# Layer norm with shifted statistics: partial mean ahead, squares summed among the output tiles

## Chip, cores and metric

The kernel runs on one core of a Trainium2 chip. The metric is the device time of one launch in microseconds; the median of several executions is compared.

## What is computed

One inference step of a trunk of four layers over 384 tokens (128 context, 256 latent) of width 1024. A layer is a token mixer (gated MLP, SSD scan, HGRN2 scan, gated MLP again) and a mixture of 16 experts. Each of the eight sub-layers ends in a layer norm:

```
def layer_norm(x, g, b):
    mu = mean(x); var = mean(square(x - mu))
    return (x - mu) * rsqrt(var + 1e-5) * g + b

for li in range(4):
    sh1, sc1, g1, sh2, sc2, g2 = modulation(cond, w_mod[li], b_mod[li])
    h = x * (1 + sc1) + sh1
    x = layer_norm(ALPHA * x + g1 * mixer(h), ln_g[li, 0], ln_b[li, 0])
    h = x * (1 + sc2) + sh2
    x = layer_norm(ALPHA * x + g2 * moe(h), ln_g[li, 1], ln_b[li, 1])
```

## The kernel before

Activations lie transposed: 128 features on the partitions, 8 tiles (`KD`) of 384 tokens (`T`). `x`, `y` (the residual sum), `h32` (the modulated input of the next sub-layer) and the pair `hh`, `hl` (high and low part of it for two-part products) are all [128, 8, 384]. Every engine has a program of its own, written out by hand; order is by program order on an engine and by counting semaphores between engines. A norm is numbered q = 2 x layer for the one behind the mixer and 2 x layer + 1 for the one behind the experts.

**Weights.** SP loads 1 MB chunks into four buffers (`raw`); load c waits until chunk c - 4 has been used. Most chunks are split: ScalarE copies the high part (`whi`), POOL subtracts it (`wlo`, L1341), TensorE multiplies three times (L1408 to L1410). Chunks of `w_mod` are summed by VectorE alone, four instructions a chunk into `macc` (`mod_chunk`, L1672 and L1675), and their end frees the buffer.

**Out projection of a mixer** (`out_tiles`). TensorE makes eight output tiles m, in banks m % 4 of PSUM, from one chunk each (gated MLP and SSD) or half a chunk (HGRN2). After a tile VectorE adds it into `y` (`residual`, L1734, which raises `y_ready`); in layers 0 and 1 VectorE does the `mod_chunk` m ahead of the residual of tile m, in layer 3 one ahead of every second tile, in layer 2 likewise. The order of loads is w_mod chunk m, then out chunk m. Tile 7 is followed on TensorE by `mod_sum` (L1442, 32 small matmuls) in mixer projections. Behind tile m TensorE does the mean step m - 1 (`mean_step`, L1450: y tile times a matrix of 1/1024, summed in bank 6). Behind the experts the projection has the same form (L1632, L1633, banks m % 3) without chunks.

**Norm.** When the mean is complete, VectorE subtracts it from all of `y` in four instructions (L1715), ScalarE squares each pair of tiles (L1225, `ln_sq`), TensorE sums the squares in bank 5 (`variance`, L1458), ScalarE takes the root (L1227, in seven of eight norms with an ACT_TABLE_LOAD ahead), VectorE the reciprocal (L1718). Then comes a loop over the tiles: VectorE multiplies (L1720) and writes `h32` in two segments of 128 and 256 tokens (`modulate`, L1705), ScalarE writes `x` (L1231) and, behind the experts, `hh` (L1235), from which POOL makes `hl` (L1354).

**Who comes next.** Behind the first norm of a layer TensorE computes the router from `h32` (L1536, three token tiles in banks 4 to 6, each with `claim`), transposes `h32` (L1527) and gathers. `claim(b, name, value)` makes TensorE wait, before it writes bank b again, for the event that the bank's last user has registered.

Of the kernel before, what the change touches and what calls it, by code (L numbers as in the profile page):

```python
# [28 lines left out]
P = 128  # L29
# [112 lines left out]
def trunk(nc, A, O):  # L142
# [11 lines left out]
    with ctx:  # L154
# [54 lines left out]
        sq = ar("ln_sq", [P, KD, T], F32, 0)  # L209
# [98 lines left out]
        def bank(b):  # L308
# [6 lines left out]
            h32_ready hh_ready hl_ready y_ready mean_done diff_ready sq_ready var_done std_ready norm_ready x_ready  # L315
# [889 lines left out]
        def _(act):  # L1205
# [16 lines left out]
            def layer_norm(q, last=False):  # L1222
                for j in range(4):
                    act.wait_ge(S["diff_ready"], 4 * q + j + 1)
                    act.activation(sq[:, 2 * j:2 * j + 2, :], y[:, 2 * j:2 * j + 2, :], ACT.Square).then_inc(S["sq_ready"], 1)  # L1225
                act.wait_ge(S["var_done"], q + 1)
                act.activation(std[:, :], bank(5), ACT.Sqrt, bias=eps[:, 0:1]).then_inc(S["std_ready"], 1)  # L1227
                l, w = q // 2, q % 2
                for k in range(KD):
                    act.wait_ge(S["norm_ready"], 8 * q + k + 1)  # L1230
                    act.activation(x[:, k, :], y[:, k, :], ACT.Identity, scale=c_("lng", (2 * l + w) * 8 + k),  # L1231
                                   bias=c_("lnb", (2 * l + w) * 8 + k)).then_inc(S["x_ready"], 1)
                    if w and not last:
                        act.wait_ge(S["h32_ready"], 8 * (q + 1) + k + 1)
                        act.activation(hh[:, k, :], h32[:, k, :], ACT.Copy).then_inc(S["hh_ready"], 1)  # L1235
# [161 lines left out]
        def _(pe):  # L1397
# [48 lines left out]
            def mean_step(q, k):  # L1446
                pe.wait_ge(S["y_ready"], 8 * q + k + 1)
                if k == 0:
                    claim(6, "diff_ready", 4 * q + 4)
                ins = pe.matmul(bank(6), mean_d[:, :], y[:, k, :], start=(k == 0), stop=(k == KD - 1))  # L1450
                if k == KD - 1:
                    ins.then_inc(S["mean_done"], 1)

            def variance(q):
                claim(5, "std_ready", q + 1)
                for k in range(KD):
                    pe.wait_ge(S["sq_ready"], 4 * q + k // 2 + 1)
                    ins = pe.matmul(bank(5), mean_d[:, :], sq[:, k, :], start=(k == 0), stop=(k == KD - 1))  # L1458
                ins.then_inc(S["var_done"], 1)

            def out_tiles(l, rhi, rlo, halves, ready, count):

                q = 2 * l
                for m in range(KD):
# [7 lines left out]
                    if m:  # L1472
                        mean_step(q, m - 1)
                mean_step(q, KD - 1)
# [42 lines left out]
            def experts(l):  # L1517
# [15 lines left out]
                for k in range(KD):  # L1533
                    pe.wait_ge(S["h32_ready"], 8 * q + k + 1)
                    for t in range(NT):
# [91 lines left out]
                for m in range(KD):  # L1627
# [7 lines left out]
                    if m:  # L1635
                        mean_step(q, m - 1)
                mean_step(q, KD - 1)
# [4 lines left out]
            for l in range(DEPTH):  # L1642
# [6 lines left out]
                variance(2 * l)  # L1649
                experts(l)  # L1650
                variance(2 * l + 1)
# [3 lines left out]
        def _(dve):  # L1655
# [47 lines left out]
            def modulate(src, k):  # L1703
                for c, a, b in SEGS:
# [4 lines left out]
            def layer_norm(q, last=False):  # L1709
# [3 lines left out]
                dve.wait_ge(S["mean_done"], q + 1)  # L1713
                for j in range(4):
                    dve.tensor_tensor(y[:, 2 * j:2 * j + 2, :], y[:, 2 * j:2 * j + 2, :],  # L1715
                                      bank(6).unsqueeze(1).to_broadcast([P, 2, T]), ALU.subtract).then_inc(S["diff_ready"], 1)
                dve.wait_ge(S["std_ready"], q + 1)
                link(dve.reciprocal(rstd[:, :], std[:, :]))  # L1718
                for k in range(KD):
                    dve.tensor_tensor(y[:, k, :], y[:, k, :], rstd[:, :], ALU.mult).then_inc(S["norm_ready"], 1)  # L1720
                    if not last:
                        dve.wait_ge(S["norm_ready"], 8 * q + k + 1)
                        modulate(y, k)
# [7 lines left out]
            def residual(l, m, src, g_tile):  # L1731
# [4 lines left out]
                ins.then_inc(S["y_ready"], 1)  # L1736

# [269 lines left out]
```

## Time and profile before

| | us |
|---|---|
| Median of 3 runs | 3290.02 (3288.75 to 3301.81) |
| Profiled execution | 3285.35 |
| Its span on the core | 3283.6 |
| TensorE busy | 2724.3 (83%) |
| VectorE busy | 1518.5 (46%) |
| ScalarE busy | 744.5 (23%) |
| POOL busy | 802.0 (24%) |

TensorE's busy time counts overlapping matmuls and says little alone. The profile's timeline, read around each norm, shows which engine waits for which; the granted clock of TensorE (1.00 is 2.4 GHz, 0.50 is 1.2 GHz) stands in the last columns of a table by stretches. An fp32 matmul shows as two records.

### The profile page before, as it was taken

To read this page: it belongs to the slowest core of one execution; us is meant where nothing else is said; L and a number is where in the kernel's file an instruction comes from. 1 tells how busy PE (TensorE), PEld (TensorE's weight loads), DVE (VectorE), ACT (ScalarE), POOL (GpSimd) and SP (SyncE) were. 2 spreads that over 40 slices of the span, in tenths; PEclk is the share of its full clock that TensorE was granted. 3 is DMA by queue.
4 is the path that set the end of the run, shared out by engine and by line. 5 is a ranking of instruction groups with operands and counts; after the bars stand their busy time and mean duration, and the time that the engine had idled before them with its cause. 6 is when DMAs were issued, how large, how long until landed. Compare 5 with 4: busy or idle time off the path is not lost.

```text
span 3283.6 us, 30539 instructions
## 1 busy us (share of the span) xinstructions
PE 2724.3 (83%) x11846; PEld 1982.1 (60%) x11846; DVE 1518.5 (46%) x2423; ACT 744.5 (23%) x1252; POOL 802.0 (24%) x501
## 2 busy tenths in 40 slices
PE   1788998887986778889898876678888889989997
PEld 1688853445975667744347865567544469975444
DVE  7546532234546766522234567767322332662002
ACT  0132220002442332300013332332100033321101
POOL 2255200002442234100003555633000025630000
PEclk9889889898897889799998875578999989989999
DMA  6534447783320114278782420013588824335883
GB/s 218 169 113 129 141 154 281 274 289 116 106 90 26 52 52 144 74 267 297 267 282 89 135 68 4 5 41 116 177 285 285 292 95 134 114 118 178 297 301 114
DMA packets 291854, 524.42 MB, mean 160 GB/s; under 512 B 9472, under 2 KB 141056, under 8 KB 291328
## 3 DMA queue, kind: packets, MB, share of 16 engines
q1 hardware_dynamic: 288256, 519.33, 46.8%
q10 hardware_dynamic: 3456, 3.15, 0.3%
q8 instruction: 95, 1.56, 0.2%
q14 instruction: 47, 0.39, 0.0%
HBM read 517.73 MB, written 4.72 MB: 159 GB/s over the span
## 4 chain that ended last, share of the span: by engine, by line
PE 61%; DVE 19%; DMA 9%; issue 5%; ACT 3%; POOL 2%; SPq 0%; ACTq 0%; DVEq 0%
PE ps L1596 14%; PE ps L1611 10%; DMA raw<-moe_w_down 6%; DVE macc L1675 6%; PE ps L1408 5%; PE ps L1409 5%; PE ps L1410 5%; PE ps L1442 3%; PE ps L627 2%; PE ps L1458 2%; PE ps L1431 1%; PE ps L1432 1%; PE ps L1433 1%; POOL wlo L1341 1%; DVE h L1705 1%
## 5 line engine op out<-in xcount | busy, mean ns | idle before, releaser
L1341 POOL TENSOR_TENSOR wlo<-raw,whi 128x1024 fp32r<-128x1024 f32 x202 | 528.2, 2630 | 1709.4 <-ACT whi L1213 1709.4
L1596 PE MATMUL ps<-raw,xg 128*128 128x512 f32 x1536 | 696.3, 597 | 0.0
L1596 PEld LDWEIGHTS ps<-raw,xg 128*128 128x128 f32 x1536 | 285.8, 192 | 323.6 <-issue 321.8
L1611 PE MATMUL ps<-raw,hidt 128*128 128x512 f32 x768 | 389.4, 655 | 109.9 <-DMA raw<-moe_w_down 107.7
L1675 DVE SCALAR_TENSOR_TENSOR macc<-raw,cond_s,macc 128x1024 f32<-128x1024 f32 x336 | 459.7, 1430 | 9.0 <-DMA raw<-w_mod 9.0
L1886 DVE SCALAR_TENSOR_TENSOR hid<-ps,cws,sg 128x256 f32<-128x256 f32 x96 | 46.5, 484 | 780.0 <-ACT sg L1306 780.0
L1611 PEld LDWEIGHTS ps<-raw,hidt 128*128 128x128 f32 x768 | 157.3, 209 | 329.9 <-issue 193.3
L1408 PE MATMUL ps<-hh,whi 128*128 128x384 f32 x832 | 293.4, 353 | 35.2 <-POOL wlo L1341 19.3
L1213 ACT ACTIVATE whi<-raw 128x1024 fp32r<-128x1024 f32 x202 | 207.0, 1054 | 400.7 <-DMA raw<-gmlp_w_out 115.1
L1410 PE MATMUL ps<-hh,wlo 128*128 128x384 f32 x832 | 284.4, 342 | 0.0
L1409 PE MATMUL ps<-hl,whi 128*128 128x384 f32 x832 | 284.4, 342 | 0.0
L1280 ACT ACTIVATE hidt<-ps 128x256 f32<-128x256 f32 x96 | 36.8, 383 | 871.2 <-PE ps L1586 871.2
L1431 PE MATMUL ps<-whi,hh 128*128 128x256 f32 x480 | 145.2, 302 | 66.1 <-POOL wlo L1341 57.5
L1408 PEld LDWEIGHTS ps<-hh,whi 128*128 128x128 f32 x832 | 161.6, 194 | 45.6 <-POOL wlo L1341 20.9
L1409 PEld LDWEIGHTS ps<-hl,whi 128*128 128x128 f32 x832 | 161.9, 195 | 1.5 <-issue 0.5
L1410 PEld LDWEIGHTS ps<-hh,wlo 128*128 128x128 f32 x832 | 160.9, 193 | 0.0
L1432 PE MATMUL ps<-whi,hl 128*128 128x256 f32 x480 | 143.2, 298 | 0.0
L1433 PE MATMUL ps<-wlo,hh 128*128 128x256 f32 x480 | 143.0, 298 | 0.0
L1431 PEld LDWEIGHTS ps<-whi,hh 128*128 128x128 f32 x480 | 100.2, 209 | 68.6 <-POOL wlo L1341 58.4
L1014 PE MATMUL ps<-uw 128*128 128x128 f32 x336 | 92.4, 448 | 56.2 <-DVE uw L1123 56.2
L1442 PE MATMUL ps<-ones,macc 128*128 128x1 f32 x768 | 99.8, 264 | 45.8 <-DVE macc L1675 45.8
L1442 PEld LDWEIGHTS ps<-ones,macc 128*128 128x128 f32 x768 | 101.4, 214 | 51.9 <-issue 31.7
(322 smaller groups left out, 4261.5 us busy)
## 6 DMA issues: line engine op xcount, KB each, us to landing
raw<-moe_w_gu SPq DMA_DIRECT2D x192, 1024.0 KB, 6.1
raw<-w_mod SPq DMA_DIRECT2D x96, 1024.0 KB, 5.3
raw<-moe_w_down SPq DMA_DIRECT2D x96, 1024.0 KB, 5.5
raw<-gmlp_w_in SPq DMA_DIRECT2D x32, 1024.0 KB, 5.7
raw<-ssd_w_in SPq DMA_DIRECT2D x21, 1024.0 KB, 5.3
raw<-hgrn_w_in SPq DMA_DIRECT2D x20, 1024.0 KB, 5.2
raw<-gmlp_w_out SPq DMA_DIRECT2D x16, 1024.0 KB, 5.7
raw<-ssd_w_out SPq DMA_DIRECT2D x8, 1024.0 KB, 5.9
```

Source lines behind the costliest of these rows:

```text
L1213: act.activation(split_sub(whi, s0), raw_sub(s0), ACT.Copy).then_inc(S["hi_ready"], 1)
L1341: pool.tensor_tensor(split_sub(wlo, s0), raw_sub(s0), split_sub(whi, s0).bitcast(F32), ALU.subtract).then_inc(S["lo_ready"], 1)
L1408: pe.matmul(out, lhi, rhi, start=first, stop=False)
L1409: pe.matmul(out, lhi, rlo, start=False, stop=False)
L1410: return pe.matmul(out, llo, rhi, start=False, stop=last)
L1431: pe.matmul(outs[t], hh[:, k, tk], pair(whi, k), start=(k == 0), stop=False)
L1432: pe.matmul(outs[t], hl[:, k, tk], pair(whi, k), start=False, stop=False)
L1433: ins = pe.matmul(outs[t], hh[:, k, tk], pair(wlo, k), start=False, stop=(k == KD - 1))
L1442: ins = pe.matmul(ps[:, 7, 2 * j + v:2 * j + v + 1], macc[:, v, j * P:(j + 1) * P], ones[:, 0:1], start=True, stop=True)
L1596: ins = pe.matmul(ps[:, s % 2, :], xg[:, w, k, :], whole(what, s, 4)[:, k % 4, :], start=(k == 0), stop=(k == KD - 1))
L1611: ins = pe.matmul(ps[:, OUT_BANKS[w % 2][h], :], hidt[:, s % 2, k, :], whole("D", s, 2)[:, k, 512 * h:512 * h + 512], start=(e == 0 and k ...
L1675: ins = dve.scalar_tensor_tensor(out=macc[:, v, :], in0=w[:, k, :], scalar=by, in1=macc[:, v, :], op0=ALU.mult, op1=ALU.add)
```

## The change

1. `shift`: after the residual of tile 4, VectorE subtracts from all eight tiles of `y` the mean of tiles 0 to 3 (twice the sum that the mean matrix gives), in four instructions of 2, 2, 1 and 3 tiles. Mean steps are left for tiles 0 to 3 only.
2. ScalarE squares tile by tile, as tiles come, into `ln_sq_...`, which has an area of its own by stage. TensorE sums the squares of tiles 0 to 3 between output tiles 6 and 7, those of tiles 4 to 7 behind tile 7, each with a step that sums y of tiles 4 to 7 in bank 4 (delta, the mean that remains). Variance is E[y^2] - delta^2: ScalarE squares delta, VectorE subtracts, ScalarE takes the root.
3. VectorE subtracts delta (`centre`) two tiles ahead of the multiply in the loop, from PSUM.
4. Behind mixers ScalarE writes the 256-token segment of `h32`, and the router waits for it (`h32b_ready`).

```diff
@@ scalar: layer_norm
-                for j in range(4):
-                    act.wait_ge(S["diff_ready"], 4 * q + j + 1)
-                    act.activation(sq[:, 2 * j:2 * j + 2, :], y[:, 2 * j:2 * j + 2, :], ACT.Square).then_inc(S["sq_ready"], 1)
-                act.wait_ge(S["var_done"], q + 1)
-                act.activation(std[:, :], bank(5), ACT.Sqrt, bias=eps[:, 0:1]).then_inc(S["std_ready"], 1)
+                for k in range(KD):
+                    if k <= 4:
+                        act.wait_ge(S["diff_ready"], 3 * q + k // 2 + 1)
+                    else:
+                        act.wait_ge(S["y_ready"], 8 * q + k + 1)
+                    act.activation(sq_of(q)[:, k, :], y[:, k, :], ACT.Square).then_inc(S["sq_ready"], 1)
+                act.wait_ge(S["delta_done"], q + 1)
+                act.activation(rstd[:, :], bank(4), ACT.Square).then_inc(S["dsq_ready"], 1)
+                act.wait_ge(S["var_read"], q + 1)
+                act.activation(std[:, :], std[:, :], ACT.Sqrt, bias=eps[:, 0:1]).then_inc(S["std_ready"], 1)
...
                     act.wait_ge(S["norm_ready"], 8 * q + k + 1)
+                    if w == 0:
+                        act.activation(h32[:, k, LC:T], y[:, k, LC:T], ACT.Identity, scale=cmod[:, 0, k, 1:2],
+                                       bias=cmod[:, 1, k, 1:2]).then_inc(S["h32b_ready"], 1)
@@ tensor
+                    claim(6, "shift_read", q + 1)
+                ins = pe.matmul(bank(6), mean_d[:, :], y[:, k, :], start=(k == 0), stop=(k == 3))
...
+            def stat_step(q, k):
+                if k >= 4:
+                    if k == 4:
+                        pe.wait_ge(S["diff_ready"], 3 * q + 3)
+                        claim(4, "delta_step", 8 * q + 8)
+                    else:
+                        pe.wait_ge(S["y_ready"], 8 * q + k + 1)
+                    ins = pe.matmul(bank(4), mean_d[:, :], y[:, k, :], start=(k == 4), stop=(k == KD - 1))
+                    if k == KD - 1:
+                        ins.then_inc(S["delta_done"], 1)
+                if k == 0:
+                    claim(5, "var_read", q + 1)
+                pe.wait_ge(S["sq_ready"], 8 * q + k + 1)
+                ins = pe.matmul(bank(5), mean_d[:, :], sq_of(q)[:, k, :], start=(k == 0), stop=(k == KD - 1))
...
+            def statistics(q, m):
+                if 1 <= m <= 4:
+                    mean_step(q, m - 1)
+                for k in {KD - 2: range(4), KD - 1: range(4, KD)}.get(m, ()):
+                    stat_step(q, k)
@@ vector: layer_norm
+                dve.wait_ge(S["dsq_ready"], q + 1)
+                dve.wait_ge(S["var_done"], q + 1)
+                dve.tensor_tensor(std[:, :], bank(5), rstd[:, :], ALU.subtract).then_inc(S["var_read"], 1)
+                def centre(k):
+                    dve.tensor_tensor(y[:, k, :], y[:, k, :], bank(4), ALU.subtract).then_inc(S["delta_step"], 1)
+                centre(0)
+                centre(1)
                 dve.wait_ge(S["std_ready"], q + 1)
                 link(dve.reciprocal(rstd[:, :], std[:, :]))
                 for k in range(KD):
+                    dve.wait_ge(S["delta_step"], 8 * q + k + 1)
                     dve.tensor_tensor(y[:, k, :], y[:, k, :], rstd[:, :], ALU.mult).then_inc(S["norm_ready"], 1)
+                    if k + 2 < KD:
+                        centre(k + 2)
...
+            def shift(q):
+                dve.wait_ge(S["y_ready"], 8 * q + 5)
+                dve.wait_ge(S["mean_done"], q + 1)
+                for a, b in ((0, 2), (2, 4), (4, 5), (5, 8)):
+                    dve.scalar_tensor_tensor(out=y[:, a:b, :], in0=bank(6).unsqueeze(1).to_broadcast([P, b - a, T]), scalar=-2.0,
+                                             in1=y[:, a:b, :], op0=ALU.mult, op1=ALU.add).then_inc(S["diff_ready" if b <= 5 else "shift_read"], 1)
```

Three places, as the instructions stand on their engines. VectorE, layer 0, before, from the residual of out tile 4 to that of tile 5 (`macc` is the sum of a w_mod chunk):

```order
L1734 SCALAR_TENSOR_TENSOR y_t<-ps,mods,y_t 128x256
L1675 SCALAR_TENSOR_TENSOR macc<-raw,cond_s,macc 128x1024 [waits mac_step,raw_in2]
L1675 SCALAR_TENSOR_TENSOR macc<-raw,cond_s,macc 128x1024 [waits mac_step] x3
L1734 SCALAR_TENSOR_TENSOR y_t<-ps,mods,y_t 128x128 [waits sub_done]
L1734 SCALAR_TENSOR_TENSOR y_t<-ps,mods,y_t 128x256
```

VectorE, the same place in the changed kernel:

```order
L1777 SCALAR_TENSOR_TENSOR y_t<-ps,mods,y_t 128x256
L1764 SCALAR_TENSOR_TENSOR y_t<-ps,y_t 128x768 [waits mean_done,y_ready]
L1764 SCALAR_TENSOR_TENSOR y_t<-ps,y_t 128x768
L1764 SCALAR_TENSOR_TENSOR y_t<-ps,y_t 128x384
L1764 SCALAR_TENSOR_TENSOR y_t<-ps,y_t 128x1152
L1701 SCALAR_TENSOR_TENSOR macc<-raw,cond_s,macc 128x1024 [waits mac_step,raw_in2,shift_read]
L1701 SCALAR_TENSOR_TENSOR macc<-raw,cond_s,macc 128x1024 [waits mac_step] x3
L1777 SCALAR_TENSOR_TENSOR y_t<-ps,mods,y_t 128x128 [waits sub_done]
```

The four instructions of the shift stand between the residual of tile 4 and the four `macc` of chunk 5.

TensorE, layer 0, behind out tile 7, before (`wrt` is the router's weight):

```order
L1442 MATMUL ps<-ones,macc 128x1 x15
L1450 MATMUL ps<-y_t,mean_d 128x384 [waits y_ready] x2
L1458 MATMUL ps<-ln_sq,mean_d 128x384 [waits sq_ready,a_ready]
L1458 MATMUL ps<-ln_sq,mean_d 128x384 [waits sq_ready] x7
L1536 MATMUL ps<-wrt,h_71 128x16 [waits router_in,below_set,diff_ready,h32_ready,std_ready,a_ready]
```

TensorE, the same place in the changed kernel:

```order
L1454 MATMUL ps<-ones,macc 128x1 x15
L1475 MATMUL ps<-y_t,mean_d 128x384 [waits a_ready,diff_ready]
L1481 MATMUL ps<-ln_sq_gmlp,mean_d 128x384 [waits sq_ready]
L1475 MATMUL ps<-y_t,mean_d 128x384 [waits y_ready]
L1481 MATMUL ps<-ln_sq_gmlp,mean_d 128x384 [waits sq_ready]
...
L1481 MATMUL ps<-ln_sq_gmlp,mean_d 128x384 [waits sq_ready]
L1566 MATMUL ps<-wrt,h_74 128x16 [waits below_set,router_in,h32_ready,shift_read,h32b_ready,var_read,delta_step]
```

Eight steps instead of ten stand between `mod_sum` and the router, and the router's first matmul has `delta_step` among its waits.

ScalarE, the first norm of layer 0, changed kernel:

```order
L1232 ACTIVATE ln_sq_gmlp<-y_t 128x384 [waits diff_ready] x5
L1232 ACTIVATE ln_sq_gmlp<-y_t 128x384 [waits y_ready] x3
L1234 ACTIVATE ln_rstd<-ps 128x384 [waits delta_done]
L1236 ACT_TABLE_LOAD
L1236 ACTIVATE ln_std<-ln_std,eps 128x384 [waits var_read]
```

The table load stands behind the Square of delta, where before it stood behind the four squares of `y`.

## Rows read from the trace of the kernel before

**Rows 1.** The page: the chain that ended last, by engine.
```profile
PE 61%; DVE 19%; DMA 9%; issue 5%; ACT 3%; POOL 2%; SPq 0%; ACTq 0%; DVEq 0%
```

**Rows 2.** Timeline, layer 0's mixer norm: start, us, engine, line, operands, count, [idle <-releaser].
```profile
388.58 2.22 PE L1450 MATMUL ps<-y_t,mean_d 128*128 128x384 f32 x4
...
390.91 3.54 DVE L1715 TENSOR_TENSOR y_t<-y_t,ps 128x768 f32<-128x768 f32 x4 [1.27 <-PE ps L1450]
...
392.88 7.00 PE L1458 MATMUL ps<-ln_sq,mean_d 128*128 128x384 f32 x16 [2.08 <-ACT ln_sq L1225]
...
395.35 1.28 ACT L1227 ACT_TABLE_LOAD   x1
...
399.92 0.58 ACT L1227 ACTIVATE ln_std<-ps,eps 128x384 f32<-128x384 f32 x1 [3.29 <-PE ps L1458]
...
400.54 2.55 DVE L1718 RECIPROCAL ln_rstd<-ln_std 128x384 f32<-128x384 f32 x1 [6.08 <-ACT ln_std L1227]
```

**Rows 3.** Timeline, norm behind layer 0's experts.
```profile
794.38 0.81 PE L1450 MATMUL ps<-y_t,mean_d 128*128 128x384 f32 x2
...
798.37 7.09 PE L1458 MATMUL ps<-ln_sq,mean_d 128*128 128x384 f32 x16 [2.08 <-ACT ln_sq L1225]
```

**Rows 4.** Stretches: us; PE, PEld, DVE, ACT, POOL busy (count); clock; DMA; GB/s.
```profile
389.40:396.10 6.70, 4.62 (x8) 2.09 (x7) 3.75 (x6) 4.13 (x5) 0.00 (x0) 0.50 0.32 126
396.20:399.90 3.70, 3.69 (x12) 1.88 (x10) 0.00 (x0) 0.43 (x1) 0.00 (x0) 1.00 0.00 0
1272.85:1283.95 11.10, 11.08 (x51) 10.84 (x52) 1.51 (x2) 2.00 (x2) 7.91 (x3) 0.82 0.40 122
1314.30:1322.75 8.45, 8.45 (x50) 8.45 (x50) 7.51 (x7) 2.01 (x2) 3.31 (x2) 1.00 0.60 181
```

**Rows 5.** Timeline of ScalarE, a table load with its inputs ready.
```profile
217.35 1.28 ACT L1260 ACT_TABLE_LOAD   x1
218.64 0.49 ACT L1260 ACTIVATE gu<-ps 128x384 f32<-128x384 f32 x1
```

**Rows 6.** Timelines of VectorE, SP, POOL and ScalarE, layer 0, out tiles 5 and 6.
```profile
358.85 4.87 DVE L1675 SCALAR_TENSOR_TENSOR macc<-raw,cond_s,macc 128x1024 f32<-128x1024 f32 x4
...
363.74 0.37 SPq L350 DMA_DIRECT2D raw<-w_mod  x1
...
367.15 0.37 SPq L350 DMA_DIRECT2D raw<-gmlp_w_out  x1
...
364.89 4.74 POOL L1341 TENSOR_TENSOR wlo<-raw,whi 128x1024 fp32r<-128x1024 f32 x2 [9.97 <-ACT whi L1213]
...
372.73 2.01 ACT L1213 ACTIVATE whi<-raw 128x1024 fp32r<-128x1024 f32 x2 [6.97 <-DMA raw<-gmlp_w_out]
```

**Rows 7.** Timeline of VectorE, layer 3, out tile 5.
```profile
2893.28 13.07 DVE L1675 SCALAR_TENSOR_TENSOR macc<-raw,cond_s,macc 128x1024 f32<-128x1024 f32 x4
```

**Rows 8.** Waits in layer 1's out projection: engine, line, releaser: total, times, longest us.
```profile
PE ps L1408 <- POOL wlo L1341: 7.6, 2, 6.9
```

**Rows 9.** Timeline of TensorE, router and transposes of layer 0.
```profile
404.53 6.55 PE L1536 MATMUL ps<-wrt,h 128*128 128x16 f32 x30 [4.64 <-DVE h L1705]
...
410.92 2.80 PE L1527 MATMUL ps<-ident,h 128*128 128x128 f32 x12
...
413.51 3.86 PE L1536 MATMUL ps<-wrt,h 128*128 128x16 f32 x18
```

**Rows 10.** Timelines of VectorE and POOL, loop of the norm behind layer 0's experts.
```profile
810.47 1.34 DVE L1705 TENSOR_SCALAR h<-y_t,cmod 128x128 f32<-128x128 f32 x2
...
812.31 1.34 DVE L1705 TENSOR_SCALAR h<-y_t,cmod 128x128 f32<-128x128 f32 x2
...
812.45 1.06 POOL L1354 TENSOR_TENSOR hl<-h,hh 128x384 fp32r<-128x384 f32 x1 [0.78 <-ACT hh L1235]
```

**Rows 11.** Timeline, the last norm of the kernel.
```profile
3272.56 3.84 DVE L1720 TENSOR_TENSOR y_t<-y_t,ln_rstd 128x384 f32<-128x384 f32 x8
3273.15 4.90 ACT L1231 ACTIVATE x_t<-y_t,cols 128x384 f32<-128x384 f32 x8 [3.21 <-DVE y_t L1720]
```

More of the change, by code:

```diff
@@ L207, in trunk, with sq_of @@
         AR = place[0]
-        sq = ar("ln_sq", [P, KD, T], F32, 0)
+        sqs = {name: ar("ln_sq_" + name, [P, KD, T], F32, kb) for name, kb in (("gmlp", 3), ("ssd", 3), ("hgrn", 0), ("moe", 57))}
+        def sq_of(q):
+            return sqs["moe" if q % 2 else ("gmlp", "ssd", "hgrn")[q // 2 % 3]]
         h32 = ar("h32", [P, KD, T], F32, 12)
@@ L1448, in mean_step @@
                 if k == 0:
-                    claim(6, "diff_ready", 4 * q + 4)
-                ins = pe.matmul(bank(6), mean_d[:, :], y[:, k, :], start=(k == 0), stop=(k == KD - 1))
-                if k == KD - 1:
[L1452 to L1459, printed above, removed]
+                    claim(6, "shift_read", q + 1)
+                ins = pe.matmul(bank(6), mean_d[:, :], y[:, k, :], start=(k == 0), stop=(k == 3))
+                if k == 3:
+                    ins.then_inc(S["mean_done"], 1)
+            def stat_step(q, k):
[12 more added lines that the diff above has]
+                ins = pe.matmul(bank(5), mean_d[:, :], sq_of(q)[:, k, :], start=(k == 0), stop=(k == KD - 1))
+                if k == KD - 1:
+                    ins.then_inc(S["var_done"], 1)
+            def statistics(q, m):
[3 more added lines that the diff above has]
+                    stat_step(q, k)
             def out_tiles(l, rhi, rlo, halves, ready, count):
@@ L1471, in out_tiles @@
                         mod_sum(group)
[L1472 to L1474 removed]
+                    statistics(q, m)
             def gmlp(l):
@@ L1701, in prepare_scale, with modulate @@
                 link(dve.tensor_tensor(cmod[:, 0, :, :], cmod[:, 0, :, :], g, ALU.mult))
-            def modulate(src, k):
-                for c, a, b in SEGS:
+            def modulate(src, k, segs=SEGS):
+                for c, a, b in segs:
                     ins = dve.tensor_scalar(h32[:, k, a:b], src[:, k, a:b], cmod[:, 0, k, c:c + 1], cmod[:, 1, k, c:c + 1],
@@ L1712, in layer_norm @@
                     prepare_scale(l, q % 2)
[L1713 to L1716, printed above, removed]
+                dve.wait_ge(S["dsq_ready"], q + 1)
[5 more added lines that the diff above has]
+                centre(1)
                 dve.wait_ge(S["std_ready"], q + 1)
@@ L1736, in residual @@
                 ins.then_inc(S["y_ready"], 1)
+                if m == 4:
+                    shift(2 * l + (g_tile == 40))
             def gmlp(l):
```

12 lines of the change are left out of this document (5 added, 7 removed).

## The prediction

> **What bounds the kernel now.** I read the page first, for its chain of work that ended last: TensorE holds 61% of it, VectorE 19%, transfers 9%, ScalarE 3% [rows 1]. One core runs the layers strictly in series, so what counts is the stretch around each of the eight layer norms, where nothing else can run. The timeline of such a stretch [rows 2] shows it as a relay. TensorE's last two mean steps start at 388.58, VectorE subtracts the mean from 390.91 (3.54 us), TensorE sums the squares from 392.88 (7.00 us), the square root starts at 399.92, the reciprocal at 400.54 and takes 2.55. So from the moment TensorE is free for the norm to the square root it takes 11.34 us. Behind the experts it is 794.38 to 805.50 (798.37 + 7.09, and 0.04 as from 399.88 to 399.92) [rows 2, 3], 11.12 us. The change attacks this relay. It can lose in three other places: the out projection, into which it moves work, the loop behind the reciprocal, and whoever waits for a PSUM bank.
>
> A 128x384 fp32 matmul against the mean matrix ("a step") shows as two records. At the full granted clock twelve records take 3.69 us, 0.31 each; where the granted clock is 0.50 it took about twice that [rows 4]. A step is thus 0.64 us at 2.4 GHz and 1.28 us at 1.2 GHz.
>
> **Tails, the gain.** The number of steps stays at 16 a norm. Before, two mean steps and eight square steps follow the out projection; now eight steps do (delta and squares of tiles 4 to 7), and four square steps moved ahead of tile 7. The pass over y and the Square relay leave the path. Behind the last delta matmul the new path is: Square of the delta, then the table load, then Sqrt. The load was hidden (395.35, while ScalarE waited until 399.92 [rows 2]). Now it stands behind an operation that comes late, in seven of eight norms. I cost the Square as the Sqrt of the same shape, 0.58, and the load at 1.28. The new subtraction on VectorE (about 0.55) ends before the load does, and the first two centring steps run under Sqrt.
> - Behind the experts: 14 records x 0.32 = 4.5, + 0.2 to land, + 0.58 + 1.28 + 0.08 = 6.6 against 11.1. Gain 4.5, four times: 18.0.
> - Behind the mixers the granted clock is at its low level when TensorE arrives, as in the first row of [rows 4]. I take 5 records at 0.64 and 9 at 0.32, 6.1 + 2.1 = 8.2 against 11.34: gain 3.1, three times. The fourth (layer 1) has no load but then waits for the two centring steps: 3.7. Together 13.0. With all records at the high level it would be 4.8 each, with all at the low one 0.3 each.
>
> Tails together: -31.0.
>
> On the load the Trainium skill differs. First the rows: a load ends at 218.63 and the ACTIVATE behind it starts at 218.64 [rows 5], so a switch costs 1.28 us. The Trainium skill (ScalarE: Activation LUTs, What ACT_TABLE_LOAD costs) adds a drain of about 1.38 us to the 1283 ns of the load. By that page the sum would be 7 x 1.38 = 9.7 us higher. The trace does not show this drain.
>
> **Out projection, the moved work.** After the experts and in layer 2 TensorE is the limit, and two more steps lie ahead of the end (before: six mean steps there; now four mean and four square steps): 2 x 0.64 = 1.3 each, five times: 6.4. In layer 3 TensorE waits for weights before tile 7 anyway, which hides them; 0.4.
>
> In layers 0 and 1 it is worse, because of what is queued behind the shift on VectorE. Before, VectorE does the tile-4 residual and goes straight to the four macc instructions of chunk 5: 358.85 to 363.72. The moment they end (363.74) SP issues the next w_mod load, since those macc free its buffer, and behind it, at 367.15, the last gmlp_w_out load. That lands at 372.73, 5.6 us later, and wlo is ready for tile 7 just in time [rows 6]. Now the shift comes between, eight tiles, as much as the old pass: 3.54 us [rows 2]. The macc start at about 362.5. POOL's wlo pair, which comes at 364.89 [rows 6] and did not meet them before, now falls on them. Where the two meet they alternate whole instructions: four macc take 13.07 us instead of 4.87 [rows 7]. So two macc (to 365.0), POOL 2.37, macc 1.1, POOL 2.37, macc 1.1: 371.9, which is 8.2 later than 363.7. The w_mod load then leaves at 371.9 and the gmlp_w_out load right behind it. From the issue of the first of these two loads to the landing of the second it took 9.0 us (363.74 to 372.73), so the landing is at 380.9. ScalarE 1.1 and POOL 2.4 follow, and VectorE's next macc hold POOL up by up to 1.1: tile 7 starts at 385.5, not 376.7. That is +8.8; layer 1 has the same order of loads, and I take the same. TensorE stands idle for some 7 us, and a tile that followed a wait of 6.9 us [rows 8] took 11.10 us at a granted clock of 0.82, against 8.45 at 1.00 [rows 4]: +2.6 more. I take 11.4 each, 22.8 for both. Ends: 1.3 each if macc and loads keep pace, 15 each if the clock stays low over the whole tile.
>
> Out projections together: +29.6.
>
> **The loop behind the reciprocal.** Per tile VectorE multiplies, now centres the tile after next (reads PSUM), and modulates. A multiply in a row costs 3.84/8 = 0.48 [rows 11], the centring as much.
> - First norm of a layer: multiply 0.47, centre 0.47, 128 columns of modulation 0.26: 1.20 a tile against 1.18. ScalarE gets the other 256 columns beside x, at most 2 x 0.61 [rows 11] = 1.22. No loss from pace. But the order shows a new wait: the router's first matmul writes bank 4, which the centring reads until its eighth instruction. That is in the loop's sixth pass: 5 x 1.20 + 0.47 + 0.55 = 7.0 us after the loop starts. Before, the router starts 1.4 us after it (404.53 against 403.12 [rows 2, 9]). Its 30 records take 6.55, paced by TensorE (0.21 each at the low clock), then come transposes (2.6) and 18 records (3.9) [rows 9]. All of it starts 5.6 later and nothing of it gets shorter: queued behind that one wait are router, transposes, routing and gather, and VectorE and ScalarE wait for them. +5.6, four times: 22.4. Ends: 3 each where the clock is back at 2.4 GHz in the last 18 records, 7 where it falls lower than before.
> - Second norm, three times: before, a pass takes 1.84 (810.47 to 812.31), because the modulation (1.34 for two instructions) waits for POOL's hl (1.06) [rows 10], POOL for ScalarE's hh, and this for the modulation. The centring puts the first part of the modulation behind POOL too: some 2.2 a pass for five passes, 1.75, and 0.45 before the first: 2.2, together 6.6. Ends 0.5 and 4 each.
> - Last norm: before, x is the pace, 0.61 x 8 (4.90) [rows 11]. Now multiply and centre are, 0.94 for six passes; the last x ends 7.55 after the loop's start, not 5.5: +2.1.
>
> Loops together: +31.1.
>
> **Sum.** -31.0 + 29.6 + 31.1 = +29.7 us. The profiled execution took 3285.35 us (span 3283.6), which gives 3315.0. The median of the three runs shown is 3290.02, 4.7 above it. I predict against the median: **3319.7**, +0.9%.
>
> **Rivals.**
> 1. *VectorE has room (not slower).* Place: layers 0 and 1, tile 5. If the macc of chunk 5 end before the out5 tile does (367.15), the load order is as before, and each layer costs 1.3, not 11.4: 3299.5. It decides by whether POOL's pair meets the macc; shift to macc start at 362.5 needs 4.9, and POOL comes 2.4 after. For it: POOL may be let in only later. Against: 13.07 us in layer 3. Chance 0.14.
> 2. *The clock holds (not slower).* With TensorE's steps in one run the level may stay at 2.4 GHz through norm and router. Records at 0.31 instead of 0.64 give the tails 7 more, and the router's 48 records and the transposes at half the time take the 22.4 to about 1: 3291. It decides if the granted clock between reciprocal and gather is over 0.9. Against: TensorE idles about 12 us before the router, where 4.6 us before [rows 9] already left it at the low level. Chance 0.06. With rival 1 too it is 3271, faster: 0.06, with what I may not see.
> 3. *The router's wait is hidden* (something else would hold routing as long, as the load before its Sigmoid): 3297. Against: x (8 x 1.22), tokens (3 x 0.6) and the load are done 13.5 after the loop's start, the router only at 19.9. Chance 0.06.
> 4. *The clock stays low in the tails and after the stalls*: 2.8 x 4 in the tails and 2 x 2 in the tiles: 3335. Chance 0.08.
> 5. *A table switch costs 2.66*: seven loads, 9.7 more, 3329. The rows speak against it: 0.03.
> 6. *The change does no good even in its own place*, since the delta steps wait for late squares: the eight tails gain 1 each, 3343. ScalarE is idle there for some 17 us, so 0.02.
>
> **How the numbers follow.** The forecast has 0.55: its own terms move it within 3307 to 3333. The limit of what a measurement can tell is 0.5%, 16.5 us: 3273.6 and 3306.5. Slower: 0.55 + 0.08 + 0.03 + 0.02 = 0.68. Within: rivals 1 to 3, 0.14 + 0.06 + 0.06 = 0.26. Faster: rivals 1 and 2 together, 0.06. The range takes in rivals 1, 3 and 4: 3294 to 3336.
>
> **What would show it.** In the trace of after: Sqrt about 8 us (mixers) and 6.6 us (experts) behind TensorE's first step of the tail, with the load directly behind the Square of the delta. A gap of some 7 us on TensorE before tile 7 in layers 0 and 1, ended by wlo, and the w_mod issue at 372 instead of 363.7. The router's first matmul 7.0 us after the first multiply, released by the eighth centring. Passes of 2.2 us in the second norms. If the gap is absent, rival 1 holds; if the router starts at 1.4, the bank wait is misread; either would put the time under 3300.

## The result and the profile after

| | before | changed |
|---|---|---|
| median of the runs, us | 3293.35 (14 runs) | 3314.05 (14 runs) |
| lowest to highest | 3287.6 to 3306.65 | 3303.73 to 3331.6 |
| profiled execution, its span | 3285.35, 3283.6 | 3310.71, 3308.6 |

The ratio is 1.0065, 95% interval 1.0048 to 1.0081: slower. The forecast median was 3319.7, 5.7 us above the measured one. The forecast was +29.7 us on the profiled execution; it is +25.4 there and +20.7 between the medians. A second set of runs of the same two programs gave 3322.14 against 3292.51, ratio 1.0095 [1.0068, 1.0122]; one of the 14 executions of the kernel before took 5417.91 us in that set and is not counted. So the size is known to some 10 us only, and the second experiment section says why.

The two spans differ by 25.0 us. I cut both traces at each norm's residuals, square root and first multiply (eight norms, numbered in order of time):

| part | forecast | measured |
|---|---|---|
| tails, last residual to Sqrt | -31.0 | -3.0 -4.6 -6.8 -4.6 -3.1 -4.6 -4.7 -4.5 = -36.0 |
| out projections, residual of tile 4 to that of tile 7 | +29.6 | +10.6 +1.3 +11.1 +1.3 +0.7 +1.3 +3.4 +1.3 = +30.9 |
| first multiply to the next residual (or the end) | +31.1 | -0.4 -0.3 +6.7 +2.8 +8.6 +2.9 +7.9 +2.0 = +30.2 |

The -0.4 of layer 0 in the last line hides a router that ends 4.0 later, since the expert stage behind it was 4.0 us shorter (301.0 against 305.0, first to last SiLU), which the change doesn't explain. In layers 0 to 2 this line of the table thus holds differences between executions of some 4 us a stage; only in layer 3 does the expert stage repeat (238.5 in every trace), and there +7.9 is the router's 7.4 and little else.

**The tail.** The timeline of layer 0's mixer norm (the columns of [rows 2], TensorE first, then ScalarE, then VectorE) answers to [rows 2]:

```profile
403.02 0.81 PE L1475 MATMUL ps<-y_t,mean_d 128*128 128x384 f32 x2
...
404.96 0.81 PE L1481 MATMUL ps<-ln_sq_gmlp,mean_d 128*128 128x384 f32 x2
...
405.16 0.49 ACT L1234 ACTIVATE ln_rstd<-ps 128x384 f32<-128x384 f32 x1 [8.48 <-PE ps L1475]
405.67 1.28 ACT L1236 ACT_TABLE_LOAD   x1
406.96 0.61 ACT L1236 ACTIVATE ln_std<-ln_std,eps 128x384 f32<-128x384 f32 x1
...
405.90 0.56 DVE L1741 TENSOR_TENSOR ln_std<-ps,ln_rstd 128x384 f32<-128x384 f32 x1 [6.18 <-PE ps L1481]
406.38 1.01 DVE L1744 TENSOR_TENSOR y_t<-y_t,ps 128x384 f32<-128x384 f32 x2
407.61 2.55 DVE L1749 RECIPROCAL ln_rstd<-ln_std 128x384 f32<-128x384 f32 x1 [0.22 <-ACT ln_std L1236]
```

The relay of [rows 2] is gone. The load now stands between the Square of the delta and the Sqrt, and VectorE's subtraction ends (406.46) before the load does (406.95).

**Layer 0, tiles 5 to 7.** VectorE, SP, POOL, ScalarE and TensorE, against [rows 6]:

```profile
358.41 3.55 DVE L1764 SCALAR_TENSOR_TENSOR y_t<-ps,y_t 128x768 f32<-128x768 f32 x4
362.00 9.17 DVE L1701 SCALAR_TENSOR_TENSOR macc<-raw,cond_s,macc 128x1024 f32<-128x1024 f32 x4
...
371.20 0.37 SPq L354 DMA_DIRECT2D raw<-w_mod  x1
371.61 0.47 SPq L354 DMA_DIRECT2D raw<-gmlp_w_out  x1
...
364.34 5.75 POOL L1353 TENSOR_TENSOR wlo<-raw,whi 128x1024 fp32r<-128x1024 f32 x2 [9.94 <-ACT whi L1217]
...
380.02 2.00 ACT L1217 ACTIVATE whi<-raw 128x1024 fp32r<-128x1024 f32 x2 [14.81 <-DMA raw<-gmlp_w_out]
381.93 2.99 ACT L1232 ACTIVATE ln_sq_gmlp<-y_t 128x384 f32<-128x384 f32 x7
...
382.58 4.28 PE L1481 MATMUL ps<-ln_sq_gmlp,mean_d 128*128 128x384 f32 x8 [7.13 <-ACT ln_sq_gmlp L1232]
```

The four macc of tile 5 take 9.17 us instead of 4.87, since POOL's pair falls on them. Both loads leave at 371.20 and 371.61 (363.74 and 367.15 before), and the last high halves come at 380.02 instead of 372.73. One row was not in the forecast: ScalarE does all squares behind those high halves, and TensorE, whose steps 0 to 3 stand ahead of tile 7, waits 7.13 us for the squares, not for its weights.

**Layer 3.** ScalarE and TensorE at the same place:

```profile
2931.98 2.00 ACT L1217 ACTIVATE whi<-raw 128x1024 fp32r<-128x1024 f32 x2 [15.09 <-DMA raw<-gmlp_w_out]
2933.89 2.99 ACT L1232 ACTIVATE ln_sq_gmlp<-y_t 128x384 f32<-128x384 f32 x7
...
2934.54 4.51 PE L1481 MATMUL ps<-ln_sq_gmlp,mean_d 128*128 128x384 f32 x8 [2.35 <-ACT ln_sq_gmlp L1232]
```

**The router** of layer 0 starts 7.0 us after the first multiply (410.20), released by the centring (L1744), and against [rows 9]:

```profile
417.22 6.58 PE L1566 MATMUL ps<-wrt,h 128*128 128x16 f32 x30 [11.46 <-DVE y_t L1744]
...
426.24 2.21 PE L1566 MATMUL ps<-wrt,h 128*128 128x16 f32 x18
```

In all four layers it starts 7.0 us after the multiply (1.4 before). It ends 4.0, 5.6, 7.3 and 7.4 later than before.

**Second norms.** A pass of the loop behind layer 0's experts, VectorE and POOL, against [rows 10]:

```profile
814.03 0.55 DVE L1744 TENSOR_TENSOR y_t<-y_t,ps 128x384 f32<-128x384 f32 x1
...
814.28 1.00 POOL L1366 TENSOR_TENSOR hl<-h,hh 128x384 fp32r<-128x384 f32 x1 [21.29 <-ACT hh L1247]
814.49 1.19 DVE L1731 TENSOR_SCALAR h<-y_t,cmod 128x128 f32<-128x128 f32 x2
...
816.54 1.19 DVE L1731 TENSOR_SCALAR h<-y_t,cmod 128x128 f32<-128x128 f32 x2
```

A pass takes 2.05 (814.49 to 816.54), where the forecast had 2.2 and before 1.84.

### The profile page after: what moved, and what is told of

Same layout as the page of the kernel before. It is cut to its first block, busy times and chain, and to the rows that moved or that the text cites. A ratio compares the mean times of both kernels' runs of the same rounds, so it can differ in the third digit from the quotient of the medians.

```text
span 3308.6 us, 30709 instructions
## 1 busy us (share of the span) xinstructions
PE 2719.3 (82%) x11846; PEld 1987.7 (60%) x11846; DVE 1538.1 (46%) x2463; ACT 768.0 (23%) x1324; POOL 805.0 (24%) x501
## 4 chain that ended last, share of the span: by engine, by line
PE 61%; DVE 20%; DMA 9%; issue 5%; ACT 3%; POOL 2%; SPq 0%; ACTq 0%; DVEq 0%
PE ps L1626 14%; PE ps L1641 9%; DMA raw<-moe_w_down 6%; DVE macc L1701 6%; PE ps L1420 5%; PE ps L1422 5%; PE ps L1421 5%; PE ps L1454 3%; PE ps L631 2%; PE ps L1443 2%; PE ps L1444 1%; PE ps L1445 1%; PE ps L1481 1%; POOL wlo L1353 1%; DVE uw L1127 1%
## 5 line engine op out<-in xcount | busy, mean ns | idle before, releaser
L1420 PE MATMUL ps<-hh,whi 128*128 128x384 f32 x832 | 293.6, 353 | 36.8 <-POOL wlo L1353 18.3
L1420 PEld LDWEIGHTS ps<-hh,whi 128*128 128x128 f32 x832 | 161.6, 194 | 47.3 <-POOL wlo L1353 19.9
```

The lines of the kernel that those rows point to most:

```text
L1420: pe.matmul(out, lhi, rhi, start=first, stop=False)
```

## Experiments: the two causes, taken away and put in

My theory: two things of equal weight eat the tails' gain and the rest. One is the wait of the router for PSUM bank 4, the other the shift ahead of tile 5's mod chunk, which delays the loads behind it. The main rival: these waits fill time in which something else would be waited for, and what costs is spread over loops and moved steps. The kernel before is at 3293.61 us for the first four. All ratios are to the kernel before in the same set of runs; "first set" and "second set" are the two ratios of the changed kernel, 1.0065 and 1.0095.

**The router out of bank 4.**

```diff
-                    claim(4 + t, "route_ready", l + 1)
+                    claim(5 + t, "route_ready", l + 1)
...
-                        ins = pe.matmul(ps[:, 4 + t, 0:NE], h32[:, k, toks(t)], wrt[:, k, :], start=(k == 0), stop=(k == KD - 1))
+                        ins = pe.matmul(ps[:, 5 + t, 0:NE], h32[:, k, toks(t)], wrt[:, k, :], start=(k == 0), stop=(k == KD - 1))
...
-                act.activation(rt[:, 0, :, :], ps[:, 4:4 + NT, 0:NE], ACT.Sigmoid).then_inc(S["route_ready"], 1)
+                act.activation(rt[:, 0, :, :], ps[:, 5:5 + NT, 0:NE], ACT.Sigmoid).then_inc(S["route_ready"], 1)
```

> Changed kernel, but the router writes banks 5, 6 and 7 instead of 4, 5 and 6, so that its first matmul no longer waits for the eighth centring. Theory (the wait for bank 4 costs its full length in every layer): the router starts 1.2 us after the loop starts, not 7.0, and ends at 12.5 to 14.5, not 18.3 to 19.9; 4 x 5.6 = 22 us less than the changed kernel's 3314, so about 3292, level with before. Rival (the clock or the expert stage behind it gives the wait back, as layer 0 of the trace hints, where the loop's start to the next residual was 0.4 us shorter than before in spite of the wait): within 6 us of 3314.

Measured: 3299.96, ratio 1.0029 [1.0011, 1.0046]. TensorE's wait ahead of the router is now for the modulated tile:

```profile
417.98 6.55 PE L1566 MATMUL ps<-wrt,h 128*128 128x16 f32 x30 [5.96 <-DVE h L1731]
```

The router starts 1.5 us after the multiply in every layer, and it ends 3.9, 5.5, 5.5 and 5.5 us earlier (some 20.5 in sum). In time it gives 12 us against the first set of the changed kernel and 22 against the second. The traced execution itself took 3310.93, 11 above its median, with an out projection of 39.2 in layer 0 and an expert stage of 309.2 in layer 1, so its total says nothing here. Layer 3 does, as its expert stage repeats: from the first multiply to the next residual it takes 300.5 us, against 306.7 in the changed kernel and 305.0 in the second execution of that. So there the wait is paid in full; over all four layers the time says 12 to 22 us.

**The shift behind the mod chunk.** The changed kernel, with `shift` just ahead of the residual of tile 5.

```diff
-                if m == 4:
-                    shift(2 * l + (g_tile == 40))
...
+                if m == 5:
+                    shift(2 * l)
...
+                    if m == 5:
+                        shift(2 * l + 1)
```

> Changed kernel, but the shift stands behind the four macc instructions of w_mod chunk 5 (just ahead of the residual of tile 5), not ahead of them. Theory (the shift delays the macc, these the load of the next w_mod chunk and of the last out chunk): in layers 0 and 1 the macc take 4.9 again, the w_mod load leaves some 8 us earlier, and residual 4 to residual 7 takes about 29 to 30 us, not 37.7 and 38.9; layer 3 hardly changes; 16 to 19 us less than 3314, so 3295 to 3298. Rival (TensorE stands for the squares of tiles 0 to 3, which ScalarE does only behind its last whi, and the place of the shift does not matter): the stretch stays over 35 us and the time within 5 us of 3314.

Measured: 3297.84, ratio 1.0011 [0.9995, 1.0027]: 18 us under the first set. VectorE and SP in layer 0:

```profile
360.18 4.87 DVE L1701 SCALAR_TENSOR_TENSOR macc<-raw,cond_s,macc 128x1024 f32<-128x1024 f32 x4
364.97 3.54 DVE L1766 SCALAR_TENSOR_TENSOR y_t<-ps,y_t 128x768 f32<-128x768 f32 x4
...
365.08 0.37 SPq L354 DMA_DIRECT2D raw<-w_mod  x1
368.47 0.37 SPq L354 DMA_DIRECT2D raw<-gmlp_w_out  x1
```

The macc have their 4.87 again and the w_mod load leaves as they end. Residual 4 to 7 takes 28.8 and 29.1 in layers 0 and 1 (37.7 and 39.0 in the changed kernel), and layer 3 stays at 35.1. From the first residual to the last, layers 0 and 1 are 8.9 and 9.9 us shorter than in the changed kernel, 18.8 in sum.

**Both moves.** Both diffs above.

> Both edits, router in banks 5 to 7 and the shift behind chunk 5. If the two costs are separate and additive: 38 to 41 us less than the changed kernel, 3273 to 3276, which is 17 to 20 us faster than before (ratio 0.994 to 0.995). If one hides the other: the better of the two single edits, 3292 to 3298.

Measured: 3281.88, ratio 0.9967 [0.9954, 0.998]. With 0.36% and 0.54% of the single moves against the first set the sum would be 0.90%; it is 0.98%. Against the second set it is 1.28% where 1.50% would be the sum. Each of these differences is known to some 0.2 to 0.3% only. What is clear of that is that neither loss hides the other (0.62% and 0.44% under the single moves), and that without them the change is faster than the kernel before.

**The kernel before, with the router's wait put in.**

```diff
+                pe.wait_ge(S["norm_ready"], 8 * (q - 1) + 7)
                 for k in range(KD):
```

> Kernel before, with one added wait: TensorE starts the router only when seven tiles are multiplied, some 6.2 us later than now. Nothing else changes. Theory (the router is on the path in all four layers): the router starts at 7.6 after the loop's start; 6.2 x 4 = 25 us more than before's 3293, about 3318; less where the clock has risen by the end of the router. Rival (given back in the expert stage): under 8 us more.

Measured: 3317.16, ratio 1.0068 [1.0041, 1.0095], 22 us more. TensorE in layer 0, against [rows 9]:

```profile
411.89 6.55 PE L1537 MATMUL ps<-wrt,h 128*128 128x16 f32 x30 [11.08 <-DVE y_t L1721]
```

The router ends 6.4, 6.4, 6.7 and 6.6 us later, 26 in sum; the time has 22, with an interval of 9 us to either side, and layer 3's stage from the multiply to the next residual grows from 298.8 to 305.4. The wait costs that without any other part of the change, so the rival, that something else would hold routing (under 8 us), is out.

**The kernel before, with the shift's load on VectorE.** Four scratch instructions with the shift's shapes, whose result nothing reads, ahead of the residual of tile 4 in layers 0, 1 and 3; VectorE waits for their end, as it does for the shift's.

```diff
+                if m == 4 and g_tile == 16 and l != 2:
+                    dve.wait_ge(S["y_ready"], 16 * l + 4)
+                    for a, b in ((0, 2), (2, 4), (4, 5), (5, 8)):
+                        dve.scalar_tensor_tensor(out=scr[:, a:b, :], in0=bank(0).unsqueeze(1).to_broadcast([P, b - a, T]), scalar=-2.0,
+                                                 in1=y[:, a:b, :], op0=ALU.mult, op1=ALU.add).then_inc(S["scr_done"], 1)
+                    dve.wait_ge(S["scr_done"], 4 * (l + 1 - (l > 2)))
```

> The kernel before, with four scratch instructions on VectorE behind out tile 4 of layers 0, 1 and 3: the shapes and sources of the shift (a PSUM bank and tiles of y in), their result goes to an area that nothing reads. They hold up residual 4 and the mod chunk behind it, and no square, no product and no bank depend on them. My theory (the shift meets POOL's half products, the mod chunk behind it then runs late, and the transfer that waits for its raw buffer is late by that): residual 4 to 7 grows by 9 to 11 us in layers 0 and 1 as in the changed kernel (27.1 to 37.7, 27.9 to 39.0), by less than 1 us in layer 3 (31.8), and the time goes up by 18 to 22 us, to 3311 to 3316. The rival (the squares that ScalarE does only behind its last high halves make the 10 us, the late transfer is covered): under 5 us more in each layer and under 8 us in sum.

Measured: 3310.99 against 3296.19, ratio 1.0051 [1.0034, 1.0069]: 15 us more, between the two expectations and nearer to the theory. Layer 0, VectorE, SP, ScalarE:

```profile
359.18 3.55 DVE L1736 SCALAR_TENSOR_TENSOR scr<-ps,y_t 128x768 f32<-128x768 f32 x4 [7.90 <-PE ps L1411]
362.76 0.74 DVE L1741 SCALAR_TENSOR_TENSOR y_t<-ps,mods,y_t 128x128 f32<-128x128 f32 x2
363.42 6.98 DVE L1676 SCALAR_TENSOR_TENSOR macc<-raw,cond_s,macc 128x1024 f32<-128x1024 f32 x4
...
370.43 0.37 SPq L351 DMA_DIRECT2D raw<-w_mod  x1
370.84 0.47 SPq L351 DMA_DIRECT2D raw<-gmlp_w_out  x1
...
379.33 2.00 ACT L1214 ACTIVATE whi<-raw 128x1024 fp32r<-128x1024 f32 x2 [12.34 <-DMA raw<-gmlp_w_out]
```

The macc meet POOL, both loads leave together, and the last high halves come at 379.33, with no statistics step moved. My expectation counted from residual 4, which here is itself 3.6 late, so residual 4 to 7 grew by 4.0 and 7.1 only and fell by 3.5 in layer 3. From the first residual to the last it is +7.6, +10.8 and +0.3 us in layers 0, 1 and 3: 18.3 in layers 0 and 1, where the changed kernel has 21.5 by the same count. So the late load makes up most of that, as the 18.8 that the second experiment took away say too. The remaining 2.7 to 3.2 us are about what two more steps a layer cost where nothing else is in the way (1.3 behind the experts). To the square root it is only +6.7 and +6.9, some 14 us, because the tails behind the late tile 7 came out 1.0 and 3.9 shorter, at a granted clock of 0.87 in both (0.75 and 0.59 in the kernel before). That fits the 15 us of the time, where the theory had 18 to 22. Tile 7 of layer 1 before, here, and in the changed kernel (the columns of [rows 4]):

```profile
1324.24:1332.64 8.40, 8.40 (x49) 8.40 (x49) 7.32 (x5) 0.00 (x0) 2.25 (x1) 1.00 0.65 235
1333.27:1344.41 11.14, 11.14 (x48) 11.14 (x49) 0.94 (x1) 0.00 (x0) 3.18 (x1) 0.73 0.32 104
1338.04:1346.66 8.62, 8.62 (x51) 8.49 (x49) 0.00 (x0) 0.00 (x0) 0.30 (x1) 1.00 0.28 109
```

After the wait tile 7 runs at a lower clock here (11.14 us), but not in the changed kernel, where four square steps stand between the wait and the tile. In layer 3 the same instructions are free. There the macc take 9.55 instead of 13.07 [rows 7], so scratch work and macc together (13.1) take what the macc alone took before: they had been waiting for POOL anyway.

## Experiments: the squares, the table, and how far one program repeats

**Squares of tiles 0 to 3 ahead of the last high halves** on ScalarE in layers 0, 1 and 3, otherwise the changed kernel.

```diff
+            early = {46: 0, 104: 2, 200: 6}
...
             def high(n):
+                if n in early:
+                    squares(early[n], range(4))
```

> The changed kernel, with the squares of tiles 0 to 3 put ahead of the last two high halves in ScalarE's order at the mixers of layers 0, 1 and 3; the shift and the router are as in the changed kernel. Theory for layer 3, which grew by 3.4 us where I had 0.4: its statistics steps 0 to 3 stand ahead of tile 7's product on TensorE and wait for squares that ScalarE starts only at 2933.89, behind its last high half; with them early, residual 4 to 7 of layer 3 falls from 35.1 to 31.8 to 32.3. In layers 0 and 1, where the last high half comes at 380, 16 us behind the one before it, residual 4 to 7 falls by 3 to 5 us each (tile 7 then waits for its own low half instead). Sum 9 to 13 us less than the changed kernel, 3301 to 3305. The rival (tile 7 waits for its weights anyway, and the squares only fill that wait): within 3 us of the changed kernel and layer 3 still at 35.

Measured: 3318.04 against 3296.19, ratio 1.0071 [1.0049, 1.0093]. ScalarE in layer 3:

```profile
2924.84 2.00 ACT L1228 ACTIVATE whi<-raw 128x1024 fp32r<-128x1024 f32 x2 [1.56 <-DMA raw<-gmlp_w_out]
2926.75 1.75 ACT L1220 ACTIVATE ln_sq_gmlp<-y_t 128x384 f32<-128x384 f32 x4
2941.65 2.01 ACT L1228 ACTIVATE whi<-raw 128x1024 fp32r<-128x1024 f32 x2 [13.14 <-DMA raw<-gmlp_w_out]
```

Residual 4 to 7 fell from 35.2 to 32.6 in layer 3, near the 31.8 to 32.3 expected, and by 3.0 and 1.6 in layers 0 and 1: 7.2 us in the trace, and nothing in the time. In layers 0 and 1 tile 7 starts 4.2 and 2.4 us earlier, counted from the first residual, but takes 9.9 us in both at a granted clock of 0.83 to 0.85, not 8.8 and 8.6 at 1.00, which gives back a part. The expert stages of layers 1 and 2 (first to last SiLU) were 309.3 and 308.2 us long, against 300.7 and 301.7. In those TensorE waits for its expert weights, and these waits explain 4.5 of layer 1's 8.6 us. The waits in one window of layer 1 (1408 to 1730), first the changed kernel, then this one:

```profile
PE ps L1641 <- DMA raw<-moe_w_down: 33.5, 11, 6.6
```
```profile
PE ps L1647 <- DMA raw<-moe_w_down: 38.0, 11, 6.7
```

Whether the kernel or the run makes these long had to be asked. So both kernels ran once more, unaltered, on one chip.

> The changed kernel once more, unaltered, on the same chip as the next one. Between the traces so far the expert stages of layers 0 to 2 (first to last SiLU) lie anywhere from 298.5 to 309.3 us, that of layer 3 is 238.5 in every one. If that is the run and not the kernel, this trace of the same program has other lengths there than its first one had (301.0, 300.7, 301.7), by 3 us or more in one layer at least, while the norms and out projections come out as before within 0.5 us. If the lengths belong to the kernel, they are the same within 0.5 us.

> The kernel with the early squares once more, unaltered, beside the changed kernel on one chip. Its mixers were 7.2 us shorter in the trace, as expected in layer 3 (32.6) and half of it in layers 0 and 1, but its time wasn't. If its long expert stages of layers 1 and 2 (309.3 and 308.2) were that run's, the median now lies 3 to 9 us under that of the changed kernel, and those stages come out shorter. If the early squares themselves make the expert stages longer, they are at 308 or more again, and the median is within 3 us of the changed kernel or above it.

| us | changed | once more | early squares | once more |
|---|---|---|---|---|
| median | 3314.05 | 3322.14 | 3318.04 | 3310.84 |
| expert stage, layer 0 | 301.0 | 302.9 | 301.9 | 299.5 |
| layer 1 | 300.7 | 303.9 | 309.3 | 305.9 |
| layer 2 | 301.7 | 300.8 | 308.2 | 304.5 |
| layer 3 | 238.5 | 238.5 | 238.5 | 238.5 |
| residual 4 to 7, layers 0, 1, 3 | 37.7 39.0 35.2 | 36.4 38.8 33.9 | 34.7 37.4 32.6 | 34.6 38.7 32.5 |
| router's end behind the multiply, layers 0 to 3 | 18.3 19.9 19.9 19.9 | 19.9 19.9 18.2 18.6 | 19.9 19.9 18.3 19.9 | 19.9 19.9 18.3 18.4 |

One program's expert stages differ by up to 3.7 us between two executions, wherever mod chunks and expert weights share the loads (layers 0 to 2). A SiLU follows the one before by 10.5 us in each of layer 3's last 22 steps; in layers 0 to 2 some of the same steps take up to 24.7 in these four traces. My "within 0.5 us" for norms and out projections was wrong too: the latter differ by 1.3 in layers 0 and 3, and layer 3's tail is 9.9 in one and 13.3 in the other. On one chip the early squares are 11.3 us under the changed kernel (1.0058 [1.004, 1.0076] against 1.0095), which is the first expectation of 9 to 13 and more than the 3 to 9 of the second; the first pair of runs has them level. Over all out projections the second pair of traces has 3.4 us, not 7.2. What is shown is layer 3 (35.2 and 33.9 without, 32.6 and 32.5 with); a gain in time is likely and no more. Both traces of the early squares are above both of the changed kernel in layers 1 and 2. But so are those of kernels without early squares: 309.2 and 304.5 with the router out of bank 4, 307.5 and 305.6 with the scratch instructions. So nothing shows that early squares make these stages longer, and nothing rules it out.

**The Sqrt table early.** Both moves, and:

```diff
+                        if k == KD - 1:
+                            act.activation(pre[:, q:q + 1], eps[:, 0:1], ACT.Sqrt)
...
                 centre(0)
-                centre(1)
...
-                    if k + 2 < KD:
-                        centre(k + 2)
+                    if k + 1 < KD:
+                        centre(k + 1)
```

> The kernel with both moves (router in banks 5 to 7, shift behind the chunk of tile 5), and in addition a Sqrt of one column ahead of the square of tile 7, so that the Sqrt table is loaded while ScalarE waits for residual 7; and only the centring of tile 0 stands ahead of the reciprocal, the others one multiply ahead in the loop. Theory: the table load of 1.28 us that now ends just ahead of the Sqrt is gone from the chain there; the chain is then the square of the delta, VectorE's subtraction, the Sqrt (0.5 to 0.9 us shorter), times 8 norms: 4 to 7 us less than the kernel with both moves, 3275 to 3278 against its 3281.9. If a table load came with every change of function (the page's 1.28 us twice and a drain), the square of tile 7 would bring the other table back, a second load would stand in the tail, and it would be 0 to 10 us slower than that kernel instead.

Measured: 3281.59, ratio 0.9961 [0.9947, 0.9975], where both moves alone had 0.9967 [0.9954, 0.998]: no gain that can be told from nothing, and not the 4 to 7 us expected. ScalarE, the norm behind layer 0's experts:

```profile
797.10 0.49 ACT L1237 ACTIVATE ln_rstd<-ps 128x384 f32<-128x384 f32 x1 [3.21 <-PE ps L1478]
798.44 0.61 ACT L1239 ACTIVATE ln_std<-ln_std,eps 128x384 f32<-128x384 f32 x1 [0.85 <-DVE ln_std L1746]
```

The load now runs at 789.42, two squares follow it, and no second load comes. Sqrt starts 1.34 us after the Square of the delta starts, not 1.80. But a tail is shorter by 0.4 to 0.5 only, the loops take 0.1 to 0.3 more each, and the last norm's loop 1.2 (probably since its centring is now one multiply ahead, not two; no run separates the two edits). That cancels more than half of it.

**All together.** Both moves, the early squares, the early table.

> The kernel with both moves, the early squares and the early table together. If the gains are what the runs so far make them, the early squares give 3.3 us in layer 3 and 1 to 2 us in each of layers 0 and 1 (they stand at 28.8 and 29.1 there against 27.1 and 27.9 before the change), the table 4 to 7 us: 3268 to 3273, 0.6 to 0.8% under the kernel before. If the gains of the tail are given back in the stage behind (by a wait that I don't see), it stays within 3 us of 3281.9.

Measured: 3279.27, ratio 0.9952 [0.9927, 0.9977], the lowest of all, though its interval overlaps that of both moves alone, and above the 3268 to 3273 expected. Layer 3's residual 4 to 7 is 32.3 (35.3 with both moves), layers 0 and 1 stand at 29.0 each, unchanged.

## Why the prediction was right, step by step

- **Tails, -31.0, measured -36.0.** Behind the experts -4.6 (forecast -4.5); -3.0 and -3.1 behind the mixers of layers 0 and 2 (forecast -3.1). The term was too small in layer 3 (-4.7) and layer 1 (-6.8, of which I had 3.7). What differs is the granted clock, which the forecast set to one mixture for all. The same tail of layer 3, from the last residual to the square root, in the two executions of the changed kernel (the columns of [rows 4], the clock third from the end):

```profile
2948.16:2957.31 9.15, 7.95 (x41) 5.49 (x40) 1.85 (x8) 2.30 (x4) 0.07 (x1) 1.00 0.36 115
2950.80:2963.31 12.51, 11.32 (x41) 7.31 (x40) 1.84 (x8) 2.30 (x3) 0.07 (x1) 0.73 0.31 94
```

At 0.84, as in layers 0 and 2 of the first execution, it is 10.84. Layer 1's tail had 0.59 before (16.62) and 0.83 after (9.77). Since the kernel before has 14.94 there in another execution (the one with the router's wait, at 0.66), some 1.7 of the 5 us is a difference between executions.
- **The load behind the Square.** The load ends at 406.95 and the Sqrt starts at 406.96. By the Trainium skill (ScalarE: Activation LUTs, What ACT_TABLE_LOAD costs) a drain of about 1.38 us would be added; this trace agrees with the 1283 ns and shows no drain, so rival 5 is out.
- **Layers 0 and 1, +22.8, measured +21.7.** The steps on VectorE, SP and ScalarE hold: loads at 371.20 (forecast 371.9), high halves at 380.02 (380.9), tile 7 at 386.4 (385.5). What TensorE waited for was forecast wrongly. I had it wait for wlo and then work through the tile at a lower clock, 2.6 us longer. It waited for squares, then did the four square steps (4.28 us) that I had counted as hidden in the middle, and then the tile at a clock of 1.00 (8.8 us, 8.4 before). The experiments give the shares: the late load costs 18.3 us when put into the kernel before and 18.8 when taken out of the changed one, of 21.5 from the first residual to the last; the rest is about the two moved steps a layer. So the late load is the main term, as forecast, but I had it some 4 us too high, and the moved steps, which I had at nothing in these layers, make up most of that: the sum was right partly by luck. The slow tile does come where the squares don't stand in between (11.14 us with the scratch instructions, layer 1). Early squares give 3.0 and 1.6 back in the first pair of traces and 1.8 and 0.1 in the second.
- **Layer 3, +0.4, measured +3.4.** This is the step that failed: "in layer 3 TensorE waits for weights before tile 7 anyway, which hides them". The wait exists, but the moved steps could not use it, since their squares stand behind the very high halves that tile 7 waits for. With the squares early, 2.6 of it went.
- **Router, +22.4.** Start at 7.0 as forecast, in all layers. End 4.0 to 7.4 later, 24.3 in sum. In time it is 12 to 22 us when taken out, and 22 when a slightly longer wait is put in (start at 7.8).
- **Loops, +6.6 for the second norms.** The pass is 2.05, not 2.2, so each loop is 1.3 longer, not 2.2: the centring (0.55, from PSUM) runs beside POOL's 1.00, and the modulation, which took 1.34 before, now takes 1.19. From the first multiply to the last hl it is 17.1, before 15.9. The last norm has +2.0 (forecast +2.1).
- **The total.** +25.0 in the spans, +29.7 forecast. The terms are 5 us apart, which is what the tails were under-sized by; with expert stages that differ by up to 4 us between executions, that the other terms meet so closely is in part chance. Rivals 1 and 2 each had a row that would show them (w_mod leaving near 363.7, the clock over 0.9 all the way between reciprocal and gather), and neither appeared; rival 3 fell with the wait taken out and put in. The clock was 0.50 over the router's first 30 records and 0.93 over its last 18:

```profile
417.20:423.60 6.40, 6.38 (x30) 6.38 (x31) 1.86 (x5) 3.02 (x6) 0.00 (x0) 0.50 0.01 3
426.20:428.40 2.20, 2.20 (x21) 2.20 (x20) 1.38 (x2) 1.91 (x3) 0.00 (x0) 0.93 0.00 0
```

## What to carry to other kernels

A statistic that is accumulated early pays in the tail what it saves there (4.6 us a norm here, behind the experts), and can lose it twice elsewhere: through the PSUM bank that it holds into the next stage, and through what is queued behind its helper instructions on VectorE. Look for the first by asking who next claims each bank that the new code reads late, for the second by following the buffer that the delayed instruction frees to the load that waits for it. And work moved into a wait is hidden only if its own inputs are not queued behind the thing waited for.

## What the runs showed of the hardware that was not expected

- The second row above: in one trace the last 18 router records of layer 0 run at a granted clock of 0.93 (2.21 us), where those of the kernel before took 3.86 [rows 9]. Router ends, and tails behind mixers, come in lengths some 1.7 us apart in executions of one kernel, and the granted clock goes with them: the tail of layers 0 and 3 takes 9.1 us at 1.00, 10.8 at 0.84 and 12.5 at 0.73.
- One program, in two executions, has expert stages up to 3.7 us apart while the stage without mod chunks repeats at 238.5. Medians of the same program in two sets of runs were 8 us apart. So a verdict on 0.3% of this kernel calls for both versions on one chip, and for a trace of each to say which stage moved.
